# The expert queries of a transformer kernel: activations stationary, weights moving in rows of 512 or 1024 columns

## What is computed

```
def expert_block(xb):                       # 128 tokens
    q = (xb @ peer_wq).reshape(128, 8, 2, 128)            # 8 heads, 2 halves of 128
    s = einsum('thcd,ckd->thck', q, peer_subkeys)
    sv, si = top_k(s, 16)                   # 16 of 128, for each half
    cand_s = sv[:, :, 0, :, None] + sv[:, :, 1, None, :]  # 256 sums
    top_s, pos = top_k(cand_s, 16)
    eidx = 16 expert numbers per head, 128 per token
    gate = softmax(top_s)
    act = gelu(einsum('ted,td->te', peer_u[eidx], xb)) * gate
    return einsum('te,ted->td', act, peer_v[eidx])
```

## Time and profile before

| | |
|---|---|
| median of 3 runs | 2600.24 us (2589.17 to 2600.66) |
| profiled execution | 2591.99 us, its span 2590.0 us |
| PE busy / DVE busy / ACT busy | 2055.9 / 1835.6 / 1145.9 us |
| gathers and the w_ada loads, queue q0 | 855.69 MB, 81.4% of the time of the 16 DMA engines |
| weights and activations, queue q1 | 123.05 MB, 13.8% |
| mean rate over the span | 378 GB/s |

### The profile page before, as it was taken

One profiled execution on the slowest core, in us unless ns is written; L12 is line 12 of the kernel. 1 busy time (PEld: TensorE's weight loads), 2 busy tenths in 40 slices (PEclk: granted clock), 3 DMA queues, 4 the chain that ended last, 5 costly groups with the idle time before them and its releaser, 6 DMA issues.

```text
span 2590.0 us, 26276 instructions
## 1 busy us (share of the span) xinstructions
PE 2055.9 (79%) x6968; PEld 1088.7 (42%) x6968; DVE 1835.6 (71%) x4200; ACT 1145.9 (44%) x3145; POOL 978.4 (38%) x916
## 2 busy tenths in 40 slices
PE   6997787778979876988677797898877887667766
PEld 2554444544445444444334344444543444333322
DVE  0147996896667779976979556684597787867776
ACT  2123474345247443744443724563244644333333
POOL 1012343333434443554342444341134443344553
PEclk9998888988989988989988999999888998798888
DMA  9588999999999999999999999998699999999997
GB/s 345 174 295 315 403 398 399 404 380 357 415 399 369 390 396 388 402 413 411 413 416 367 356 392 407 394 403 327 242 411 369 407 408 388 414 379 420 421 420 329
DMA packets 215704, 980.25 MB, mean 378 GB/s; under 512 B 17660, under 2 KB 75544, under 8 KB 117272
## 3 DMA queue, kind: packets, MB, share of 16 engines
q0 software_dynamic: 123648, 855.69, 81.4%
q1 hardware_dynamic: 91928, 123.05, 13.8%
HBM read 977.62 MB, written 1.05 MB: 378 GB/s over the span
## 4 chain that ended last, share of the span: by engine, by line
PE 34%; DVE 26%; DMA 20%; ACT 10%; issue 9%; POOL 1%; SPq 0%; POOLq 0%; DVEq 0%; ACTq 0%
DMA EXPERT<-in_peer_uv,FIX 19%; PE VS L1133 13%; PE PA L902 10%; DVE EXPERT L1876 9%; DVE ACC L1886 3%; DVE SCR L1423 2%; PE PA L930 2%; PE PB L826 2%; PE VS L855 1%; ACT L1362 1%; ACT DIAG L1377 1%; ACT WEI L1372 1%; PE PB L1123 1%; DVE SI L1828 1%; DVE SCR L1825 1%
## 5 line engine op out<-in xcount | busy, mean ns | idle before, releaser
L1133 PE MATMUL VS<-EXPERT,DIAG 128*128 128x512 f32 x2304 | 1166.4, 648 | 237.8 <-ACT DIAG L1377 236.1
L734 POOL DMA_INDIRECT EXPERT<-in_peer_uv,FIX x768 | 904.0, 1177 | 1078.1 <-PE VS L1133 733.0
L1876 DVE CUSTOM_DVE_ANT_0 EXPERT<-EXPERT,H 128x1024 f32<-128x1024 f32 x768 | 923.7, 1224 | 305.5 <-DMA EXPERT<-in_peer_uv,FIX 294.9
L1133 PEld LDWEIGHTS VS<-EXPERT,DIAG 128*128 128x128 f32 x2304 | 455.7, 208 | 810.5 <-issue 470.4
L1370 ACT ACTIVATE GEL<-DOT 128x1 f32<-128x1 f32 x768 | 155.1, 202 | 1012.8 <-DVE DOT L1876 987.1
L902 PE MATMUL PA<-WT,HT 128*128 128x512 f32 (+2 forms) x720 | 295.3, 556 | 11.2 <-issue 8.0
L1886 DVE SCALAR_TENSOR_TENSOR ACC<-EXPERT,WEI,ACC 128x1024 f32<-128x1024 f32 x192 | 246.3, 1283 | 30.8 <-ACT WEI L1372 29.6
L1377 ACT ACTIVATE DIAG<-IDN,WEI 128x128 f32<-128x128 f32 x576 | 231.4, 402 | 69.4 <-PE VS L1133 51.5
L1372 ACT ACTIVATE WEI<-GEL,GATE 128x1 f32<-128x1 f32 x768 | 226.4, 295 | 25.0
L1123 PE MATMUL PB<-HT,WT 128*128 128x128 f32 (+1 forms) x1472 | 211.2, 304 | 27.2 <-issue 26.0
L1123 PEld LDWEIGHTS PB<-HT,WT 128*128 128x128 f32 x1472 | 204.9, 216 | 51.2 <-issue 48.7
(11 more groups left out here) (194 smaller groups left out, 1714.4 us busy)
## 6 DMA issues: line engine op xcount, KB each, us to landing
EXPERT<-in_w_ada POOLq DMA_DIRECT2D x48, 1024.0 KB, 13.3
WT<-in_peer_wq SPq DMA_DIRECT2D x92, 512.0 KB
WT<-in_w_in SPq DMA_DIRECT2D x48, 512.0 KB
WT<-in_w_out SPq DMA_DIRECT2D x48, 512.0 KB
EXPERT<-in_peer_uv,FIX POOLq DMA_INDIRECT x768
WT<-in_w_in SPq DMA_DIRECT2D x16, 384.0 KB
WT<-in_w_in SPq DMA_DIRECT2D x16, 288.0 KB
WT<-in_mla_wq_up SPq DMA_DIRECT2D x4, 512.0 KB
```

Source lines behind the costliest of these rows:

```text
L734: pool.indirect_dma_start(out=EXPERT[:, j, :], out_offset=None, in_=a["peer_uv"], in_offset=bass.IndirectOffsetOnAxis(ap=FIX[:, par, j:j + ...
L1133: ins = nc.tensor.matmul(VSUM[n][:, :], DIAG[:, i, :], EXPERT[:, j, D + n * W:D + (n + 1) * W], start=first, stop=last_one)
L1876: nc.vector.tensor_tensor_reduce(out=EXPERT[:, j, 0:D], in0=EXPERT[:, j, 0:D], in1=H2[:, b % HB, :], scale=1.0, scalar=0.0, op0=ALU.mult, ...
```

## The change

Heads are now taken in groups of four or two. For a group of n heads and one tile, `ask` loads the weights in 2n parts of 512 KB: n = 4 gives one row block of 1024 columns (rows of 4 KB), n = 2 gives two row blocks of 512 columns (rows of 2 KB). The piece of `HT` is stationary and 512 columns of weights, two heads, move. Each bank of PSUM gathers two heads over all parts. ScalarE copies a bank to `QS`. `turnq` turns it by four transposes on TensorE, ScalarE copies that to `QPT`, and `score` multiplies by the sub-keys. The first two heads of the first tile of CTX in layer 0 and of LAT in layer 1 stay as they were. `pick_groups` lays the `score` and `then` stages of one group among the `ask` stages of the next; the last group's follow on their own. The costs are 15 per part and tile for `ask`, 12 for `turnq`, 45 for `score` and 40 for `then`, so `weave` deals out the slots anew in the whole program.

```diff
+def asked(l, g, group):
+
+    h0, n, ts = group
+    return [("ask", l, g, group, part) for part in range(2 * n)]
+
+def scored(l, g, group):
+
+    h0, n, ts = group
+    turns = [("turnq", l, g, group, r) for r in range(n * len(ts) // 2)]
+    picks = []
+    for h in range(h0, h0 + n):
+        for i, t in enumerate(ts):
+            head = (h, ts, i if len(ts) > 1 else (h - h0) // 2)
+            picks += [("score", l, g, head, t), ("then", l, g, head, t)]
+    return turns, picks
+
+def zipped(first, second):
+
+    out, at = [], 0
+    for n, s in enumerate(first):
+        out.append(s)
+        to = (n + 1) * len(second) // len(first)
+        out += second[at:to]
+        at = to
+    return out
+
+def pick_groups(l, g, groups, before=()):
+
+    out, before = [], list(before)
+    for group in groups:
+        turns, picks = scored(l, g, group)
+        out += (zipped(before, asked(l, g, group)) if before else asked(l, g, group)) + turns
+        before = picks
+    return out + before
+
+
 def pick_apart(l, g):
 
 
-    n = ALONE[l, g]
-    return (pick(l, g, [(h, (0,)) for h in range(n)]),
-            pick(l, g, [(h, BOTH) for h in range(n, PH)] + [(h, (1,)) for h in range(n)]))
+    if (l, g) == (0, LAT):
+        return (pick_groups(l, g, [(0, 4, (0,)), (4, 2, (0,))]),
+                pick_groups(l, g, [(6, 2, BOTH), (0, 4, (1,)), (4, 2, (1,))]))
+    single = pick(l, g, [(0, (0,)), (1, (0,))])
+    return (single[:4] + pick_groups(l, g, [(2, 2, (0,)), (4, 4, (0,))], single[4:]),
+            pick_groups(l, g, [(0, 4, (1,)), (4, 4, (1,))]))
+
+def past(stages, h, t):
+
+    return max(n for n, s in enumerate(stages) if s[0] in ("more", "then") and s[3] is not None and s[3][0] == h
+               and t == (s[4] if s[0] == "then" else s[3][1][0])) + 1
...
+        "ask": (0, 15), "turnq": (12, 0), "score": (45, 0),
...
+        return per_tile * len(s[3][2])
...
     alone, others = pick_apart(0, LAT)
-    plan += weave(plan, first[4:] + rest + outward(0, LAT, (0,)) + alone[:6], stream_of(0) + stream_of(1, 0, SLOTS - AHEAD))
-
-    joint = 2 + 4 * (PH - ALONE[0, LAT])
-    rest = alone[6:] + attention(0, LAT, 1) + outward(0, LAT, (1,)) + others[:joint]
+    plan += weave(plan, first[4:] + rest + outward(0, LAT, (0,)) + alone[:past(alone, 1, 0)], stream_of(0) + stream_of(1, 0, SLOTS - AHEAD))
+
+    joint, two = past(others, PH - 1, 1), past(others, 0, 1)
+    rest = alone[past(alone, 1, 0):] + attention(0, LAT, 1) + outward(0, LAT, (1,)) + others[:joint]
     plan += weave(plan, rest, stream_of(1, SLOTS - AHEAD) + stream_of(2, 0, SLOTS - 2 * AHEAD))
-    plan += weave(plan, others[joint:joint + 4], stream_of(2, SLOTS - 2 * AHEAD))
+    plan += weave(plan, others[joint:two], stream_of(2, SLOTS - 2 * AHEAD))
     fronts = front(1, CTX, THREE, queries=False) + front(1, LAT, (0,), keys=False) + attention_early(1, LAT, 0)
-    plan += weave(plan, others[joint + 4:] + fronts, stream_of(3, 0, SLOTS - RING))
+    plan += weave(plan, others[two:] + fronts, stream_of(3, 0, SLOTS - RING))
...
+            elif kind == "ask":
+                v, (h, n, _), part = a["peer_wq"][l].rearrange("(k p) n -> p k n", p=P), stage[3], stage[4]
+                k = HP // n
+                return [(v[:, k * part:k * (part + 1), h * HW:(h + n) * HW], k, n * HW)]
...
-                    to = WTP[:, n % WSLOTS, :, :] if k == HP else WT[:, n % WSLOTS, 0:k, 0:cols]
+                    to = (WTP[:, n % WSLOTS, :, :] if k == HP else WTR[:, n % WSLOTS, :, :] if cols == D else
+                          WT[:, n % WSLOTS, 0:k, 0:cols])
                     sp.dma_start(to, src).then_inc(piece_in[n % WSLOTS], 16)
...
+            def ask(stage):
+
+                _, l, g, (h0, n, ts), part = stage
+                rows = HP // n
+                if part == 0:
+                    held["asked"] = [fill_b() for i in range(n * len(ts) // 2)]
+                    held["asked", "n"] = rb.n
+                if part % n == 0:
+                    half_there(ts, part // n)
+                no = npiece[0] % WSLOTS
+                piece()
+                w = WTR[:, no, :, :] if rows == 1 else WT[:, no, :, :]
+                for i, bank in enumerate(held["asked"]):
+                    t, c0 = (ts[i], 0) if len(ts) > 1 else (ts[0], i * W)
+                    for k in range(rows * part, rows * (part + 1)):
+                        last = nc.tensor.matmul(bank[:, :], HT[:, k, t * P:(t + 1) * P], w[:, k % rows, c0:c0 + W],
+                                                start=(k == 0), stop=(k == KD - 1))
+                        if k == KD - 1:
+                            last.then_inc(filled_b, 1)
+                        elif k % rows == rows - 1 and bank is held["asked"][-1]:
+                            last.then_inc(piece_used, 1)
+                        if i == 0 and k % rows == 0:
+                            release()
+                if part == 2 * n - 1:
+                    owed.append((filled_b, rb.n, 1))
+
+            def turnq(stage):
+
+                _, l, g, (h0, n, ts), r = stage
+                pe.wait_ge(emptied_b, held["asked", "n"] - len(held["asked"]) + r + 1)
+                bank = fill_b()
+                turn_tiles(bank, [QS[:, r, m, :] for m in range(4)], P).then_inc(filled_b, 1)
+                held["turned", r] = rb.n
+
+            def score(stage):
+
+                _, l, g, (h, ts, r), t = stage
+                pe.wait_ge(emptied_b, held["turned", r])
+                bank = fill_a()
+                for c in range(2):
+                    last = nc.tensor.matmul(bank[:, c * P:(c + 1) * P], QPT[:, r, 2 * (h % 2) + c, :], SKT[:, 2 * l + c, :],
+                                            start=True, stop=True)
+                last.then_inc(filled_a, 1)
...
+            def ask(stage):
+                _, l, g, (h0, n, ts), part = stage
+                if part == 2 * n - 1:
+                    for r in range(n * len(ts) // 2):
+                        bank = from_b()
+                        nc.scalar.copy(QS[:, r, :, :].rearrange("p m n -> p (m n)"), bank[:, :]).then_inc(emptied_b, 1)
+
+            def turnq(stage):
+                bank = from_b()
+                nc.scalar.copy(QPT[:, stage[4], :, :].rearrange("p m n -> p (m n)"), bank[:, :]).then_inc(emptied_b, 1)
...
+            def score(stage):
+                top(stage[4])
```

23 lines of the change are left out of this document (18 added, 5 removed).

## The result

The changed kernel takes 2659.61 us, the median of 4 runs (2650.64 to 2661.89), beside 2596.6 us for the kernel before (2589.17 to 2600.66). The ratio is 1.0223, with a 95% interval from 1.0190 to 1.0256. It is slower by some 60 us, outside the predicted range, which ended at 2622. The profiled execution took 2659.88 us, its span 2657.9 us, 67.9 us longer than before.

The account below looks back on a forecast made before the run. It took DMA as the bound, balanced with VectorE in the picks. Span 2590.0 - 20.6 - 6 + 23 - 3 = 2583.4 us; with 1.99 outside the span and 8.25 to the median, 2593 us, no change; range 2566 to 2622.

Parts of the forecast that it names:

- What bounds the kernel: Whole kernel: from about 250 us on, DMA's bytes, packets and short gaps set the time; picks balance DMA and VectorE.
- Packets, -20.6 us: Query weight loads: 2 KB and 4 KB rows instead of 1 KB save 20.6 us of DMA, bounds 19.3 to 27.0.
- The falls that I asked for: Profile after: packets under 2 KB fall by about 43,000 and the share of queue q1 by 0.8 points.
- the third rival: Query weight loads: larger packets gain nothing, by the skill's 512 B rule; 2614 us, just slower; chance 0.07.
- Weights sooner, -6 us: Waits for query weights in three windows: larger packets land sooner, 6 us back of 7.2, bounds 0 and 7.2.
- TensorE, ScalarE, VectorE, round trips, 0: Picks: TensorE up at most 17 us, ScalarE 5, VectorE the same, all off the path; nothing counted for waits.
- The new deal, +23 us: Tails of the picks: VectorE outlasts DMA, the ring holds 7 us; 23 us new idle, bounds -11 and 58.
- Fewer slots in projections and attention, -3 us: Projections and attention: slots moved into the picks leave them, where TensorE is full; 3 us back, bounds 0 and 6.
- The first (the ring carries the tails): Tails of the picks: gathers in flight in the ring cover most of DMA's shortage; 2575 us, faster; chance 0.33.
- The second: Tails of the picks: they lose everything, 58 us, and the turned queries' round trips add; 2620 us, slower; chance 0.20.
- Its 43 us of new idle: Whole kernel: new DMA idle from which the slower rival decides, where the ring holds under about 3 us.

## Why the prediction was wrong, step by step

**What bounds the kernel**: right for the kernel after: DMA is full outside the holes, and VectorE sets the tails (14.22 us a head, 13.21 with less work in the right place).

**Packets, -20.6 us**: the size was right where it was used; undone in the new kernel it costs 22 us. But "this lies wholly on the path wherever DMA is full" is wrong for a comparison with the old kernel, where 4 KB rows in every piece bring 7 us instead of 23. That VectorE masks it there (14.4 us a head against DMA's 13.6) was my guess; with 5.3 slots a head, where DMA should be the longer, the gain was no larger. The falls that I asked for came: packets under 2 KB by 43,007 and queue q1 by 0.8 points. The whole packet time fell by only 4 us. q1 is 12 us down; q0, with the same packets and bytes, is 7 us up. Holes may be the reason: a gather's packet takes longer near one. The first line is q0 in the tail at 340 to 350 us, then the two queues at 460 to 470 us, both after:

```profile
q0 software_dynamic: 379, 2.74, 72.9%
```

```profile
q0 software_dynamic: 382, 2.77, 66.3%
q1 hardware_dynamic: 390, 1.42, 35.3%
```

A gather's packet took 0.729 x 10 x 16 / 379 = 308 ns beside a hole, against 280 ns in the earlier trace rows and 278 ns here among the weights. Over whole kernels the link is loose: q0 takes 2107 to 2123 us in the seventeen, not in the order of their holes. The weights' packets of 4 KB took 0.353 x 10 x 16 / 390 = 145 ns, on the line through 1 and 2 KB; by that the term was its upper bound, 27.0, and the run shows 22, with an error that doesn't tell the two apart. The Trainium skill ("DMA: Bandwidth & Descriptors", Specifications) has line rate from 512 B on; by it the rows of 1 KB would have been free. The run with 1 KB rows speaks against it, with 22 us for the same bytes: the third rival falls.

**Weights sooner, -6 us**: half right. They land 9.3 us after issue, and `ask` waits 1.2 us in all, where L1123 stood 10.40 us at once. By the same stages (200 us from the norm at 2149 us before and at 2220 after) DMA is short by 7.3 us before and 4.9 after. So some 2 of the 6 us came back: the gap at 2185 us is gone, that at 2260 to 2275 us is still there at 2330 (2.9 us) though no weights are waited for.

**TensorE, ScalarE, VectorE, round trips, 0**: right for the turns, as the run without them shows; for the copy of `QS` ahead of them only bounded, by the 18 us above. The 62 waits of 196.4 us were read wrong: they are 30 of matmuls and 32 of weight loads, 87.0 us for the matmuls. Nothing in the sum rests on that.

**The new deal, +23 us**: the step that failed; the unfilled time grew by 72. The long tails themselves were sized well. By windows they are short by 8.2 us (320 to 360), 5.3 us (590 to 630) and 8.0 us (2020 to 2050), where I had 9.3 each. What I left out is **what stands behind a tail**. I asked how much of its own shortage the ring would carry, and took that as the end of the account. But at the end of a tail most of the ring is landed experts and little is in flight (behind the second one, three gathers issued from 628 to 633 us), and the next stages are those in which GpSimd waits 7 to 13 us for a place: stat, norm, the end of a block, the first steps of attention. In the kernel before the end of block 0 was covered by the eight gathers in flight. Behind the long tails the windows are short by 8.0 us (360 to 400), 17.9 us (630 to 660) and 6.1 us (2050 to 2070). Another 16.7 us (1040 to 1080) stand in the two-head tail of layer 0, LAT, tile 0, which I had put at 0.2 us: the end of block 1 lies between its two heads. Together that is 49 us, where the same stages before have some 14 (340 to 400, 590 to 620, 1020 to 1060 and 1970 to 2010 us). With the 11 us more in 1400 to 1600 us that is 22 + 35 + 11, less the 6 us that the gaps at 335, 560 and 1945 us had before: 62 of the 72 us. For the first tail the even tails show the link: with it full, the attention behind it has no hole. For the end of block 0 the tail is one part only: the hole stays at 10 us behind an even tail, and at 12 us in the old kernel with more slots in its picks and no tail.

**Fewer slots in projections and attention, -3 us**: nothing came back that the windows show.

**The rivals.** The first (the ring carries the tails) is out. The second came nearest, with the right side and the wrong mechanism: it had the tails lose all they could, 58 us, and round trips on top. The three long tails lost 22 of the 49 us that they could, the turns nothing, and the stages behind the tails and the ends of blocks most of the rest. Its 43 us of new idle, from which it was to decide, were passed with 72.

**Open.** The kernel with groups of two and even tails has 8 us less packet time than before and 16 us more in holes. I name the ends of blocks 0 and 1 for most of that. The run with more slots in the old picks shows such a hole at the end of block 0 by itself, but is no slower, so its price in the whole kernel is open. So is the price of the first round trip. And why the old kernel hides DMA's saving even with more slots in its picks.

## What to carry to other kernels

A ring that hides one engine behind another is a store that a stretch can spend and the next one needs. When a change makes a stretch uneven, price the stretch together with the deepest barrier behind it (stages in which no place comes free), not only the stretch itself, and count two barriers in a row as one long one. Even out by each stage's real load: a stage that loses its DMA partner needs more slots, and costs that stay as they were starve it. And before cutting work to test a bound, find in the timeline the wait that it could turn into.
